# Query and key projections of an attention stage by seven half-size products, on TensorE and VectorE

## The chip, the cores and the metric

One core of one Trainium2 chip. The kernel is one launch that computes a whole inference step; its time is device microseconds. "Before" is the median of three runs, and one further execution was recorded by the hardware profiler. All arithmetic is in f32.

## The reference, cut to what matters

The step is a two-layer trunk for a prompt of 256 tokens and 8 sample tokens: a state-space mixer, experts, an attention mixer, experts, a norm. The change is in the attention mixer's projections.

```python
ATTN_PATTERNS = ((128, 1), (512, 4), (2048, 16))     # window, dilation
qkv = (h @ w_qkv).reshape(nb, L, N_ATTN_GROUPS, 3, ATTN_HEADS, ATTN_HEAD_DIM)
...
for g, (window, dil) in enumerate(ATTN_PATTERNS):
    q, k, v = qkv[:, :, g, 0], qkv[:, :, g, 1], qkv[:, :, g, 2]
    # prompt: band attention over own residue sequence; sample: over cached keys and the own one
    k_all = jnp.concatenate([buf[:, :, 0], k], axis=1)
    s = jnp.einsum('bshd,bskhd->bshk', q, k_all[:, idx]) * ATTN_SCALE
    ...
    rows.append(jnp.stack([k, v], axis=2))           # new keys and values are outputs too
y = combine_groups(outs, lams) @ w_out
```

`h` has 264 rows (256 prompt, 8 sample) of 1024, and `w_qkv` is 1024 x 9216.

## The kernel before

Activations lie channel-first: `hT` is 128 partitions x 8 channel blocks x 264 tokens. Weights stream from HBM over SyncE's queue into `ring`, six buffers of 2 MB (L669 issues those of attention); one buffer holds 512 output columns, four tiles of 128.

Attention runs in three patterns `g` of 24 tiles `i`: 8 of queries, 8 of keys, 8 of values. `qkv_tile` (line L1523) makes one tile: 8 `pe.matmul` over the channel blocks, 128 weights columns by 264 tokens, into bank `i % 2`; ScalarE's `copy_tile` (L2081, L2084; for patterns 1 and 2 with the tokens re-ordered into four lanes) copies it to `qT`, `kT` or `vT`, and counts `q_e`. The profiler records each f32 `pe.matmul` as two matmuls and two weight loads.

Behind each key tile stands `rows_job`: two transposes (L930) that turn keys back into rows, which ScalarE's `copy_rows` (L2112) copies to `KV` and GpSimd stores to the outputs (L920, L922). Job 0 of a pattern turns the sample queries (L1545); GpSimd stores them to HBM (`sample_queries`, L891), to spread them to all partitions afterwards.

In the value part, step `t` is: `scores(g, t)` (L1570) of two heads, `qkv_tile` of value tile `t` with the next row job in its middle, then `lagging(g, t)`, which does the transposes and value products of earlier heads. VectorE's part of a step is `masked` (L2732 to L2747: scale, mask, maxima), ScalarE's `exps` (L2125), VectorE's `taken_up` (L2774 to L2779). `scores(g, t)` waits until the masks of step `t - 1` are done. ScalarE's order in a step is exponents, copied rows, value tile.

The sample tokens' scores over cached keys are 20 jobs on VectorE, `cache_scores(u)`: a product of keys and queries (L2790) and a reduction (L2795), 1024 elements wide. 16 jobs are of patterns 0 and 1; the last four, of pattern 2, do two batches each. Jobs 0 to 10 run at the start of VectorE's pattern 1, jobs 11 to 19 at the start of its pattern 2, and behind them stand `own_scores(g)` (L2716) and the pattern's masks:

```python
for u in range(0, NS + EARLY_JOBS) if g == 1 else range(NS + EARLY_JOBS, len(CJOBS)) if g == 2 else ():
    cache_scores(u)
own_scores(g)
```

GpSimd issues their transfers in order: `keys(u)` (L857) when job `u - 3` is done, `query(u)` (L866) when the product of job `u - 2` is done. In pattern 1 it issues those of jobs 0 to 7, then stores the new queries and waits for that store, then issues jobs 8 to 10. In pattern 2 it issues jobs 11 to 15 and the keys of 16 to 18, stores the new queries, waits, and issues the queries of 16 to 19.

Behind attention, SyncE's queue streams the experts' weights of layer 1 (L541); its first loads wait for counts that TensorE gives at value tile 71, at the transposes of the last step and in `attention_out` (L1768).

## Time and profile before

| | |
|---|---|
| median of 3 runs | 1605.45 us (1604.89 to 1606.84) |
| profiled execution | 1606.77 us, its span 1604.7 us |
| TensorE matmuls busy | 1523.1 us, 95% of the span |
| VectorE, ScalarE, GpSimd busy | 590.1, 441.0, 132.1 us |
| attention | about 750 to 1108 us |
| granted TensorE clock, mean | 0.987 |

In a row of the timeline the first number is the start in us from the span's start and the second the time from the first start to the last end of the instructions merged in it; what stands in brackets is the idle time of the engine before it and what ended that.

### The profile page before, as it was taken

The page shows a single profiled execution, that of the slowest core. Times are in us where ns is not written, and L with a number is a line of the kernel's source. Part 1 is how long each engine was busy: PE and PEld are TensorE (multiplying, and loading weights), DVE is VectorE, ACT ScalarE, POOL GpSimd, SP SyncE. Part 2 cuts the span into 40 slices and gives each one's busy share as a digit, 9 for nine tenths or more (in the row PEclk, how much of TensorE's full clock was granted, in tenths as well). Part 3 has the DMA queues.
Part 4 walks back from the last instruction along what each step waited for, and adds up shares of the span by engine and source line. Part 5 has one row for each costly group of instructions (what it writes and reads, how often), then busy time and mean ns, then how long its engine had stood idle before and what let it go on. Part 6 is the DMA issues. An engine that isn't in the chain of part 4 may idle for free.

```text
span 1604.7 us, 23562 instructions
## 1 busy us (share of the span) xinstructions
PE 1523.1 (95%) x9111; PEld 856.0 (53%) x9111; DVE 590.1 (37%) x1380; ACT 441.0 (27%) x1232; POOL 132.1 (8%) x286
## 2 busy tenths in 40 slices
PE   9999899999998898999999999999999999898897
PEld 6877777533333333335877878766643333333232
DVE  4589983322122222214033544544421322122123
ACT  3488871211111111112143142231311111111112
POOL 1222231100000000001001202230000000000000
PEclk9999999999999999999999999999999999999999
DMA  9678776899999999999534958697899999999996
GB/s 341 219 231 270 238 240 272 294 422 414 427 424 427 428 424 429 426 423 396 191 130 143 346 170 257 170 267 300 325 424 382 426 426 424 430 425 426 428 424 258
DMA packets 112620, 542.35 MB, mean 338 GB/s; under 512 B 9452, under 2 KB 34228, under 8 KB 80242
## 3 DMA queue, kind: packets, MB, share of 16 engines
q1 hardware_dynamic: 95414, 485.20, 75.1%
q0 software_dynamic: 16800, 55.53, 11.6%
q8 instruction: 63, 1.03, 0.3%
q10 hardware_dynamic: 316, 0.37, 0.1%
q14 instruction: 27, 0.22, 0.0%
HBM read 524.81 MB, written 16.45 MB: 337 GB/s over the span
## 4 chain that ended last, share of the span: by engine, by line
PE 60%; DMA 23%; DVE 10%; ACT 3%; issue 2%; SPq 1%; POOL 0%; DVEq 0%; ACTq 0%; POOLq 0%
PE bank L1118 19%; DMA ring<-in_moe_w_gate_up 15%; PE bank L1523 10%; PE bank L1140 10%; DMA arena<-in_moe_w_gate_up 4%; PE bank L1452 4%; PE bank L1425 3%; PE bank L930 3%; DMA arena<-sample_queries 2%; PE bank L1103 2%; PE bank L1768 2%; PE bank L1129 2%; DVE arena L2636 2%; ACT arena L2125 1%; PE bank L1155 1%
## 5 line engine op out<-in xcount | busy, mean ns | idle before, releaser
L1118 PE MATMUL bank<-ring,arena 128*64 128x512 f32 x1536 | 344.3, 602 | 30.0 <-DMA ring<-in_moe_w_gate_up 30.0
L1523 PE MATMUL bank<-hT,ring 128*128 128x264 f32 x1152 | 273.5, 391 | 0.0
L1118 PEld LDWEIGHTS bank<-ring,arena 128*64 128x64 f32 x1536 | 114.2, 138 | 255.4 <-issue 251.0
L1523 PEld LDWEIGHTS bank<-hT,ring 128*128 128x128 f32 x1152 | 214.4, 191 | 38.7 <-issue 3.7
L2471 DVE TENSOR_TENSOR arena<-arena,bank 128x512 f32<-128x512 f32 x32 | 34.4, 1074 | 429.0 <-ACT arena L1896 429.0
L1140 PE MATMUL bank<-ring,arena 128*32 128x512 f32 x1536 | 169.8, 594 | 3.5 <-ACT arena L1899 1.7
L1896 ACT ACTIVATE arena<-bank 128x512 f32<-128x512 f32 x32 | 19.1, 597 | 440.5 <-PE bank L1118 440.5
L1118 PE MATMUL bank<-arena 128*64 128x512 f32 x512 | 118.4, 615 | 15.3 <-DMA arena<-in_moe_w_gate_up 15.3
L1140 PEld LDWEIGHTS bank<-ring,arena 128*32 128x32 f32 x1536 | 49.9, 110 | 106.2 <-issue 101.5
L2412 DVE SCALAR_TENSOR_TENSOR arena<-arena 128x1024 f32<-128x1024 f32 x30 | 38.5, 1284 | 179.6 <-ACT arena L1907 179.6
L2402 DVE TENSOR_TENSOR X<-X,bank 128x512 f32<-128x512 f32 x128 | 80.5, 680 | 41.9 <-PE bank L1129 41.9
L1118 PEld LDWEIGHTS bank<-arena 128*64 128x64 f32 x512 | 40.2, 141 | 91.2 <-issue 68.9
L1425 PE MATMUL bank<-hT,ring 128*128 128x264 f32 x384 | 88.6, 387 | 0.0
L930 PE MATMUL bank<-ident,arena 128*128 128x128 f32 (+7 forms) x465 | 75.4, 272 | 10.9 <-DVE arena L2607 6.5
L930 PEld LDWEIGHTS bank<-ident,arena 128*128 128x128 f32 (+7 forms) x465 | 52.6, 138 | 54.2 <-issue 19.6
L1425 PEld LDWEIGHTS bank<-hT,ring 128*128 128x128 f32 x384 | 72.3, 190 | 12.6 <-issue 0.6
L1129 PE MATMUL bank<-arena 64*128 64x512 f32 x256 | 67.9, 628 | 0.0
L1905 ACT ACTIVATE arena<-bank 128x512 f32<-128x512 f32 x32 | 19.1, 597 | 152.5 <-PE bank L1140 152.5
L1374 PE MATMUL bank<-hT,ring 128*128 128x264 f32 x256 | 60.5, 390 | 0.0
L1452 PE MATMUL bank<-arena,ring 128*128 128x264 f32 x256 | 59.4, 392 | 0.0
L1103 PEld LDWEIGHTS bank<-arena 128*128 128x128 f32 x448 | 53.0, 193 | 10.6 <-issue 10.6
L1140 PE MATMUL bank<-arena 128*32 128x512 f32 x448 | 57.7, 593 | 0.0
(368 smaller groups left out, 1609.3 us busy)
## 6 DMA issues: line engine op xcount, KB each, us to landing
ring<-in_moe_w_gate_up SPq DMA_DIRECT2D x56, 2048.0 KB, 25.8
ring<-in_moe_w_down SPq DMA_DIRECT2D x44, 2048.0 KB, 26.5
ring<-in_moe_w_gate_up SPq DMA_DIRECT2D x76, 1024.0 KB, 20.4
arena<-in_moe_w_gate_up SPq DMA_DIRECT2D x28, 2048.0 KB, 26.3
ring<-in_attn_qkv SPq DMA_DIRECT2D x18, 2048.0 KB, 11.8
arena<-in_moe_w_down SPq DMA_DIRECT2D x28, 1024.0 KB, 26.0
ring<-in_ssm_in_proj SPq DMA_DIRECT2D x10, 2048.0 KB, 15.9
arena<-in_cache_kv_w POOLq DMA_DIRECT2D x20, 512.0 KB, 8.8
```

The lines of the kernel that those rows point to most:

```text
L930: return pe.transpose(out, in_, ident[0:in_.shape[0], 0:in_.shape[0]])
L1103: mm = pe.matmul(out[:, c, :, t, :], xn_e[:, t, d * P:(d + 1) * P], Pm[:, t, :, :], start=True, stop=True)
L1118: mm = pe.matmul(bank[j][e * SLOTS:(e + 1) * SLOTS, :], Xg[:, 4 * half + k, 2 * (p % 2) + e, :], weights(2 * half + e, p)[:, k, j * DE:(j ...
L1129: pe.matmul(bank[b][:, :], CmT[r, :], ysl[r, q, :], start=True, stop=True).then_inc(s.sc, 1)
L1140: mm = pe.matmul(bank[2 + q][o:o + HALF, :], actT[:, k, i:i + HALF], down_rows(e, p, k, kept_used)[:, q * 512:(q + 1) * 512], start=(k == ...
L1374: mm = pe.matmul(bank[0][:, 0:T], wv[:, k, (t % 4) * P:(t % 4 + 1) * P], hT[:, k, :], start=(k == 0), stop=(k == DT - 1))
L1425: mm = pe.matmul(b[:, 0:T], wv[:, k, (i % 4) * P:(i % 4 + 1) * P], hT[:, k, :], start=(n == 0), stop=(n == DT - 1))
L1452: mm = pe.matmul(bank[OUT_BANK[0][d]][:, 0:T], wv[:, k, (d % 2) * P:(d % 2 + 1) * P], conv_out[:, k, :], start=(k == 0), stop=(k == XT_TIL ...
L1523: mm = pe.matmul(bank[i % 2][:, 0:T], wv[:, k, (i % 4) * P:(i % 4 + 1) * P], hT[:, k, :], start=(n == 0), stop=(n == DT - 1))
L2402: return v.tensor_tensor(xs, xs, bank[b][:, :], ALU.add)
L2412: v.scalar_tensor_tensor(out=acc_s[:, :, :], in0=ysl[:, :, :], scalar=wcol[:, bass.ds(n, 1)], in1=acc_s[:, :, :], op0=ALU.mult, op1=ALU.ad ...
L2471: v.tensor_tensor(act_r[:, :].rearrange("s (k p) -> s k p", k=4), sg[:, :].rearrange("s (p k) -> s k p", k=4), bank[1][:, :].rearrange("s ...
```

## The change

In each pattern the query and key tiles are taken in pairs `(i, i + 1)`, all but the first two of pattern 0 and the first four of patterns 1 and 2: 19 of 24 pairs. A pair is a product of 264 x 1024 tokens with 1024 x 256 weights; it is cut in halves in each of the three sizes and made of seven products of halves (Strassen's scheme in the form with 15 sums) in place of eight. A half product is 4 `pe.matmul` of 128 weight columns by 132 tokens.

- VectorE makes four sums of token halves once (`x_sums`), and four sums of weight quarters for each pair (`weight_sums`), 128 x 512 each; one is written over the quarter in `ring`.
- TensorE (`qkv_pair`) makes the seven products in two banks, some of them accumulating on others; it waits ahead of each for copies, additions and sums. Two row jobs stand inside the pairs of keys behind the first.
- ScalarE (`copy_pair`) copies three partial products to SBUF and the last result to its place; VectorE (`add_pair`) adds the other three results, 128 x 132 each.
- VectorE's order in patterns 1 and 2 is new: two cached jobs in pattern 1, one in pattern 2; the first pair's weight sums; then for each pair its additions, the next pair's sums, one cached job (in pattern 2 only up to job 15); then the jobs that are left, `own_scores`, the masks.
- Pattern 0's mask code stands behind the first sums. The sums lie in `X`, in the cached rows' buffers (`rows_in`) in pattern 0 and in `sm` and `pT` afterwards; the masks of patterns 1 and 2 are 128 columns wide in place of 384. GpSimd's order isn't changed.

```diff
+PAIRED = tuple(24 * g + i for g in range(3) for i in range(4 if g else 2, 2 * DT, 2))
+HT_ = T // 2
+PART0, ADD0, COPY0, SUM0 = CT, CT, DI // P, DI // P
...
+        masks = [m(3 * P), m(P), m(P)]
+        x_sum4 = m(DT // 2, T // 2)
+        idle_rows = X.rearrange("p t d -> p (t d)")
+        x_sums = [idle_rows[:, s * DT // 2 * HT_:(s + 1) * DT // 2 * HT_].rearrange("p (k t) -> p k t", k=DT // 2)
+                  for s in range(3)] + [x_sum4]
+        partial = idle_rows[:, 3 * DT // 2 * HT_:(3 * DT // 2 + 3) * HT_].rearrange("p (s t) -> p s t", s=3)
+        w_room = [[rows_in.rearrange("p s d -> p (s d)")[:, b * 12 * P:(b + 1) * 12 * P] for b in range(2)],
+                  [sm.rearrange("p a b c -> p (a b c)"), pT.rearrange("p a b c d -> p (a b c d)")]]
...
+        def partial_banks(i):
+            first = (i // 2 + (i < 24)) % 2
+            q, r = bank[first], bank[1 - first]
+            return q[:, 0:HT_], r[:, 0:HT_], r[:, 2 * P:2 * P + HT_]
+        def w_sum(i, s):
+            room = w_room[i >= 24][PAIRED.index(i) % 2].rearrange("p (s k n) -> p s k n", s=3, k=DT // 2)
+            return room[:, s]
...
+            def qkv_pair(i, jobs):
+                n = PAIRED.index(i)
+                q, r, p = partial_banks(i)
+                summed = SUM0 + 8 + 4 * (n - 1)
+                if i % 4 == 0:
+                    slot = (STREAM_SLOT[1] + i // 4) % RING
+                    pe.wait_ge(loads[1][slot], 16 * (i // 4 // RING + 1))
+                def product(out, ws, xs, more=False):
+                    for k in range(DT // 2):
+                        mm = pe.matmul(out, ws[:, k, :], xs[:, k, :], start=(k == 0 and not more),
+                                       stop=(k == DT // 2 - 1), skip_group_check=more)
+                    return mm
+                if n:
+                    pe.wait_ge(s_cv, ADD0 + 3 * n)
+                pe.wait_ge(q_e, i - 1 if i - 2 not in PAIRED else i - 2)
+                product(q, quarter_of(i, 0, 0), tokens_of(0, 0)).then_inc(s_prj, 1)
+                pe.wait_ge(q_e, i)
+                pe.wait_ge(s_xdt, summed + 2 if n else SUM0 + 3)
+                product(r, quarter_of(i, 0, 1), x_sums[0]).then_inc(s_prj, 1)
+                if jobs:
+                    rows_job(*jobs[0])
+                pe.wait_ge(s_zc, COPY0 + 3 * n + 1)
+                pe.wait_ge(s_xdt, summed + 3 if n else SUM0 + 5)
+                product(q, w_sum(i, 0), x_sums[1], True).then_inc(s_prj, 1)
+                pe.wait_ge(s_zc, COPY0 + 3 * n + 2)
+                pe.wait_ge(s_xdt, summed + 3 if n else SUM0 + 6)
+                product(r, quarter_of(i, 1, 1), x_sums[3], True).then_inc(s_prj, 1)
+                pe.wait_ge(s_zc, COPY0 + 3 * n + 3)
+                pe.wait_ge(s_xdt, summed + 3 if n else SUM0 + 7)
+                product(q, w_sum(i, 1), x_sums[2], True).then_inc(s_prj, 1)
+                if jobs:
+                    rows_job(*jobs[1])
+                pe.wait_ge(s_cv, ADD0 + 3 * n + 1)
+                product(p, quarter_of(i, 1, 0), tokens_of(0, 1)).then_inc(s_prj, 1)
+                pe.wait_ge(s_cv, ADD0 + 3 * n + 2)
+                pe.wait_ge(s_xdt, summed + 4 if n else SUM0 + 8)
+                product(q, w_sum(i, 2), tokens_of(1, 1), True).then_inc(q_p, 2)
...
-                for t in range(DT):
+                for t in range(4 if g else 2):
                     qkv_tile(24 * g + t, (g - 1, 2 * DT) if g == NGRP - 1 and t == 0 else None)
                     if g and t < 2:
                         lagging(g - 1, DT + t)
                     elif g == 1 and t == 2:
                         sums_to_lanes()
-                for t in range(DT):
-                    qkv_tile(24 * g + DT + t)
-                    if g == 0 and t == 0:
+                for i in range(4 if g else 2, 2 * DT, 2):
+                    j = i - DT - 1
+                    qkv_pair(24 * g + i, ((g, j), (g, j + 1)) if j > 0 else None)
+                    if i == DT:
                         pe.wait_ge(c_v, 1)
-                    rows_job(g, t)
+                        rows_job(g, 0)
                 for t in range(DT):
                     scores(g, t)
+                    if t == 0:
+                        rows_job(g, DT - 1)
                     qkv_tile(24 * g + 2 * DT + t, (g, DT + t) if g else None)
                     lagging(g, t)
...
+            def copy_pair(i, jobs):
+                n = PAIRED.index(i)
+                q, r, p = partial_banks(i)
+                parts = partial
+                if n:
+                    act.wait_ge(s_cv, ADD0 + 3 * n)
+                act.wait_ge(s_prj, PART0 + 6 * n + 1)
+                act.activation(parts[:, 0], q, ACT.Copy).then_inc(s_zc, 1)
+                act.wait_ge(s_prj, PART0 + 6 * n + 2)
+                act.activation(parts[:, 1], r, ACT.Copy).then_inc(s_zc, 1)
+                if jobs:
+                    copy_rows(*jobs[0])
+                act.wait_ge(s_prj, PART0 + 6 * n + 3)
+                act.activation(parts[:, 2], q, ACT.Copy).then_inc(s_zc, 1)
+                if jobs:
+                    copy_rows(*jobs[1])
+                act.wait_ge(q_p, i + 2)
+                act.wait_ge(s_cv, ADD0 + 3 * n + 3)
+                for out, part in projected(i, 1):
+                    ins = act.activation(out, part(q), ACT.Copy)
+                ins.then_inc(q_e, 2)
...
+            halves_summed = [SUM0]
+            def half_sum(out, x, y, op):
+                halves_summed[0] += 1
+                v.tensor_tensor(out, x, y, op).then_inc(s_xdt, 1)
+            def sums_done():
+                v.wait_ge(s_xdt, halves_summed[0])
+            def weights_landed(i):
+                slot = (STREAM_SLOT[1] + i // 4) % RING
+                v.wait_ge(loads[1][slot], 16 * (i // 4 // RING + 1))
+                n = PAIRED.index(i)
+                if n >= 2:
+                    v.wait_ge(q_p, PAIRED[n - 2] + 2)
+            def weight_sums(i, step):
+                b11, b12, b21, b22 = (quarter_of(i, r, c) for r in range(2) for c in range(2))
+                t2, t3, t4 = (w_sum(i, j) for j in range(3))
+                if step == 0:
+                    half_sum(t3, b22, b12, ALU.subtract)
+                elif step == 1:
+                    half_sum(b12, b12, b11, ALU.subtract)
+                elif step == 2:
+                    half_sum(t2, b22, b12, ALU.subtract)
+                else:
+                    half_sum(t4, b21, t2, ALU.subtract)
+            def all_weight_sums(i):
+                weights_landed(i)
+                for step in range(4):
+                    weight_sums(i, step)
+                    if 0 < step < 3:
+                        sums_done()
+            def added(i, r, x, y):
+                for out, part in projected(i, r):
+                    ins = v.tensor_tensor(out, part(x), part(y), ALU.add)
+                ins.then_inc(s_cv, 1)
+            def add_pair(i):
+                n = PAIRED.index(i)
+                q, r, p = partial_banks(i)
+                parts = partial
+                v.wait_ge(s_zc, COPY0 + 3 * n + 3)
+                v.wait_ge(s_prj, PART0 + 6 * n + 4)
+                added(i + 1, 0, r, parts[:, 2])
+                v.wait_ge(s_prj, PART0 + 6 * n + 5)
+                added(i + 1, 1, q, parts[:, 1])
+                v.wait_ge(s_prj, PART0 + 6 * n + 6)
+                added(i, 0, p, parts[:, 0])
+            v.wait_ge(n_ht, HT_BASE[2] + DT)
+            half_sum(x_sums[0], tokens_of(1, 0), tokens_of(1, 1), ALU.add)
+            weights_landed(PAIRED[0])
+            weight_sums(PAIRED[0], 0)
+            weight_sums(PAIRED[0], 1)
+            sums_done()
+            half_sum(x_sums[1], x_sums[0], tokens_of(0, 0), ALU.subtract)
+            weight_sums(PAIRED[0], 2)
+            sums_done()
+            half_sum(x_sums[3], tokens_of(0, 1), x_sums[1], ALU.subtract)
+            half_sum(x_sums[2], tokens_of(0, 0), tokens_of(1, 0), ALU.subtract)
+            weight_sums(PAIRED[0], 3)
...
-                for u in range(0, NS + EARLY_JOBS) if g == 1 else range(NS + EARLY_JOBS, len(CJOBS)) if g == 2 else ():
+                jobs = list(range(0, NS + EARLY_JOBS) if g == 1 else range(NS + EARLY_JOBS, len(CJOBS)) if g == 2 else ())
+                ahead = 2 if g == 1 else 1
+                for u in jobs[:ahead]:
+                    cache_scores(u)
+                jobs = jobs[ahead:]
+                if g:
+                    all_weight_sums(24 * g + 4)
+                for i in range(4 if g else 2, 2 * DT, 2):
+                    add_pair(24 * g + i)
+                    if i + 2 < 2 * DT:
+                        all_weight_sums(24 * g + i + 2)
+                    if jobs and (g == 1 or jobs[0] < 2 * NS):
+                        cache_scores(jobs.pop(0))
+                for u in jobs:
                     cache_scores(u)
```

## Rows read from the trace of the kernel before

**Rows 1.** Page, parts 1, 2 and 5: engine (its matmuls); GB/s of 40 slices; groups.

```profile
PE 1523.1 (95%) x9111; PEld 856.0 (53%) x9111; DVE 590.1 (37%) x1380; ACT 441.0 (27%) x1232; POOL 132.1 (8%) x286
...
GB/s 341 219 231 270 238 240 272 294 422 414 427 424 427 428 424 429 426 423 396 191 130 143 346 170 257 170 267 300 325 424 382 426 426 424 430 425 426 428 424 258
...
L1523 PEld LDWEIGHTS bank<-hT,ring 128*128 128x128 f32 x1152 | 214.4, 191 | 38.7 <-issue 3.7
...
L930 PE MATMUL bank<-ident,arena 128*128 128x128 f32 (+7 forms) x465 | 75.4, 272 | 10.9 <-DVE arena L2607 6.5
```

**Rows 2.** Timeline, SyncE's queue after attention: start us, us, what was issued.

```profile
1094.94 4.19 SPq L541 DMA_DIRECT2D ring<-in_moe_w_gate_up  x4
```

**Rows 3.** Windows: stretch, its length, each engine's busy us (instructions), clock, DMA.

```profile
880.90:925.80 44.90, 44.90 (x209) 37.72 (x207) 22.46 (x19) 7.69 (x34) 10.25 (x19) 1.00 0.95 347
987.75:1032.60 44.85, 44.85 (x209) 37.71 (x207) 19.44 (x16) 7.65 (x33) 11.58 (x22) 1.00 0.88 248
1100.79:1104.68 3.89, 3.89 (x14) 2.96 (x10) 1.29 (x3) 0.00 (x0) 0.00 (x0) 0.50 1.01 423
```

**Rows 4.** The chain that ended last, in order of time, attention's pattern 2.

```profile
1007.72 7.91 DMA sample_queries<-X
```

**Rows 5.** Timeline, TensorE: start us, us from first start to last end, count.

```profile
73.16 0.83 PE L1354 MATMUL bank<-arena 128*128 128x128 f32 x6
...
788.87 3.73 PE L1523 MATMUL bank<-hT,ring 128*128 128x264 f32 x16
```

**Rows 6.** Groups of 750 to 1110 us by form, VectorE: busy us, mean ns.

```profile
L2790 DVE TENSOR_TENSOR arena<-arena 128x1024 f32<-128x1024 f32 x20 | 24.5, 1226 | 49.5 <-DMA arena<-sample_queries 49.4
L2795 DVE TENSOR_REDUCE arena<-arena 128x16 f32<-128x1024 f32 x16 | 19.5, 1221 | 0.6
...
L2760 DVE TENSOR_TENSOR arena<-arena 128x256 f32<-128x256 f32 x8 | 3.3, 417 | 0.0
```

**Rows 7.** Waits, 750 to 1110 us: who for whom, us, times, longest.

```profile
DVE arena L2716 <- ACT arena L2084: 54.1, 1, 54.1
```

**Rows 8.** Timeline, VectorE: start us, us, operation, idle before it and releaser.

```profile
878.17 1.23 DVE L2790 TENSOR_TENSOR arena<-arena 128x1024 f32<-128x1024 f32 x1 [0.55 <-DMA arena<-sample_queries]
...
885.00 1.23 DVE L2790 TENSOR_TENSOR arena<-arena 128x1024 f32<-128x1024 f32 x1 [1.85 <-DMA arena<-sample_queries]
...
927.53 0.22 DVE L2716 TENSOR_TENSOR arena<-arena 128x64 f32<-128x64 f32 x1
...
1003.94 1.23 DVE L2790 TENSOR_TENSOR arena<-arena 128x1024 f32<-128x1024 f32 x1 [3.42 <-DMA arena<-sample_queries]
...
1020.78 1.23 DVE L2790 TENSOR_TENSOR arena<-arena 128x1024 f32<-128x1024 f32 x1 [14.37 <-DMA arena<-sample_queries]
...
1036.47 0.23 DVE L2716 TENSOR_TENSOR arena<-arena 128x64 f32<-128x64 f32 x1
```

**Rows 9.** Timeline, TensorE, at the scores L1570 and in the clock's dip.

```profile
925.84 0.46 PE L1570 MATMUL bank<-arena 64*64 64x64 f32 x16
...
930.76 0.46 PE L1570 MATMUL bank<-arena 64*64 64x64 f32 x16
...
1037.60 0.46 PE L1570 MATMUL bank<-arena 64*64 64x64 f32 x16
...
1100.79 3.89 PE L1768 MATMUL bank<-arena,ring 128*128 128x264 f32 x8
```

**Rows 10.** Timeline, GpSimd: issues of cached keys, queries and the queries' store.

```profile
879.70 0.53 POOL L866 DMA_DIRECT2D arena<-sample_queries  x1 [7.24 <-DVE arena L2790]
...
902.00 0.61 POOL L891 DMA_DIRECT2D sample_queries<-X  x1
908.95 0.54 POOL L857 DMA_DIRECT2D arena<-in_cache_kv_w  x1 [6.34 <-DMA sample_queries<-X]
```

**Rows 11.** DMA issues by line: count, KB each, median us from issue to landing.

```profile
arena<-sample_queries POOLq DMA_DIRECT2D x16, 512.0 KB, 7.9
```

**Rows 12.** Timeline, ScalarE, pattern 1, the copy that waits for the stored rows.

```profile
936.67 0.39 ACT L2112 ACTIVATE arena<-bank 128x256 f32<-128x256 f32 x1 [2.01 <-DMA out<-X]
```

More of the change, by code:

```diff
@@ L274, in bass_hybrid_step @@
         pT = m(2, 2, 3, P)
-        mask = m(NGRP, 3 * P)
         rows_in = m(CSLOTS, D)
@@ L828, in _ @@
             for g in range(NGRP):
-                link(pool.memset(mask[:, g, :], 0.0))
+                link(pool.memset(masks[g], 0.0))
                 for c0, c1, base in ((0, P, 0), (P, 3 * P, P)) if g == 0 else ((0, P, 0),):
-                    v_ = mask[:, g, c0:c1]
+                    v_ = masks[g][:, c0:c1]
                     link(pool.affine_select(out=v_, in_=v_, compare_op=ALU.is_ge, fill=NEG, base=base,
@@ L2164, in _ @@
             for g in range(NGRP):
-                for t in range(DT):
+                for t in range(4 if g else 2):
                     if g == NGRP - 1 and t == 0:
@@ L2170, in _ @@
                         lagging(g - 1, DT + t)
-                own_columns(g, 0)
-                for t in range(DT):
-                    copy_tile(g, DT + t)
-                    copy_rows(g, t)
+                for i in range(4 if g else 2, 2 * DT, 2):
+                    j = i - DT - 1
+                    if i == DT:
+                        own_columns(g, 0)
+                    copy_pair(24 * g + i, ((g, j), (g, j + 1)) if j > 0 else None)
+                    if i == DT:
+                        copy_rows(g, 0)
+                copy_rows(g, DT - 1)
                 own_columns(g, 1)
@@ L2696, in _ @@
+            weight_sums(PAIRED[0], 3)
             v.wait_ge(s_const, 9)
-            v.tensor_copy(mask[:, 0, 0:1], mask[:, 0, 0:1]).then_inc(a_mv, 1)
+            v.tensor_copy(masks[0][:, 0:1], masks[0][:, 0:1]).then_inc(a_mv, 1)
             dist, rest, apart = pT[:, 0, 0, 0, :], pT[:, 0, 1, 0, :], sm[:, 0, 0, 0:P]
@@ L2703, in _ @@
                 link(v.tensor_scalar(apart, apart, 0.0, NEG, ALU.not_equal, ALU.mult))
-                link(v.tensor_tensor(mask[:, g, 0:P], mask[:, g, 0:P], apart, ALU.min))
-                v.tensor_copy(mask[LQ:P, g, 0:LQ], mask[LQ:P, g, LQ:P]).then_inc(a_mv, 1)
+                link(v.tensor_tensor(masks[g][:, 0:P], masks[g][:, 0:P], apart, ALU.min))
+                v.tensor_copy(masks[g][LQ:P, 0:LQ], masks[g][LQ:P, LQ:P]).then_inc(a_mv, 1)
             v.wait_ge(a_mv, 3)
@@ L2736, in masked @@
                         v.scalar_tensor_tensor(out=s_[:, h, :], in0=bank[2 + h][:, 0:3 * P], scalar=SCALE,
-                                               in1=mask[:, g, :], op0=ALU.mult, op1=ALU.add).then_inc(h_m, 1)
+                                               in1=masks[g][:, :], op0=ALU.mult, op1=ALU.add).then_inc(h_m, 1)
                 v.wait_ge(h_m, 2 * n + 2)
```

25 lines of the change are left out of this document (20 added, 5 removed).

## The prediction

> **What bounds the kernel now.** I read the page first. TensorE is busy 95% of the span, and its projection line L1523 stands there with 1152 weight loads, one ahead of each matmul, two matmuls for each `pe.matmul` of the code [rows 1]. The row of GB/s shows where DMA is the limit: the slices of both expert stages stand at 380 to 430, those of attention at 130 to 350. So attention, about 750 to 1108 us, is TensorE's, and the expert stage behind it is a stream that starts when attention gives up its buffers: the queue's first expert load of layer 1 goes out at 1094.94 [rows 2]. A shift of attention's end moves everything behind it by as much, and a shift inside attention is what has to be found.
>
> Then the table of windows, for the two stretches that hold the paired tiles of patterns 1 and 2: TensorE is busy for all of both, at granted clock 1.00, and VectorE for half (22.5 of 44.9 us, 19.4 of 44.85) [rows 3]. That half is the cached key jobs. TensorE being full hides that VectorE's half is itself nearly on the path: the chain that ended last runs in pattern 2 not through TensorE but through the transfers of the cached jobs, 7.91 us for the store of the new queries among them [rows 4]. What VectorE's program does last before the value tiles decides when these can go on.
>
> **The change, term by term.**
>
> *The products.* A run of 6 matmuls with 128 columns lasts 0.83 us, one of 16 with 264 columns 3.73 [rows 5]. A single one of 128 lasts 0.27 (line L930 [rows 1]), so they start (0.83 - 0.27)/5 = 0.11 us apart and drain for 0.16 after that; for 264 it is (3.73 - 0.16)/16 = 0.223. For 132 columns I take 0.1125 (the row of 128 gives 0.11, a line between the two 0.115). One product is 4 `pe.matmul`, 8 matmuls, 0.90 us; a pair is 7 products, 6.30 us, in place of 32 x 0.223 = 7.12. If nothing waits the gain is 0.82 us a pair, 15.6 us for 19: the most the change can bring.
>
> In all the rows that these steps come from a weight load (0.19 us each [rows 1]) stands ahead of every matmul and adds nothing to the step; for 132 columns I see no reason for another case. The Trainium skill (TensorE: Matmul & The Clock Gate, Part 3, The mechanism) says that a weight load overlaps a running matmul only where it goes to another row group. By that rule the load would lie open and the change would be dear; this trace doesn't agree, since the steps of 0.11 and 0.223 hold the loads already.
>
> *Each product's wait.* Ahead of a product TensorE waits for a copy or an addition of the product before last, so each has one product, 0.90 us, of cover. A drain (0.17), a 132-column copy or addition (VectorE's 256-column form takes 0.417 and the 1024-column one 1.226 [rows 6], so about 0.29 for 132, and I take 0.39 where the columns go to lanes) and the way back (about 0.1) make 0.6 to 0.7: hidden. The closest one is the second product of the next pair, which wants two weight sums: 0.20 after the sixth product the last addition starts, 0.30 for it, then 0.60 and 0.69 (512 columns between the same two forms), together 1.84 against 1.80. I take 0.04 a pair.
>
> *Pattern 0* (7 pairs): VectorE has nothing else here (its first wait for a copied tile is 54.1 us [rows 7]). 6 x (7.12 - 6.34) + 0.82 = **-5.5 us**. The mask code, some 4 us of small steps, now stands behind eight sums of some 5 us, and is through about when the first addition is wanted.
>
> *Pattern 1, to the end of the key tiles.* VectorE does two cached jobs, then the sums of the first pair. A job is 1.226 + 1.221 and a step between, 2.49 us [rows 6]. They start at 878.17 [rows 8] (all times here as before, without pattern 0's gain), end at 883.15, two sums are there at 884.45. TensorE comes to pair 28 at 880.9, where the first stretch of [rows 3] begins, and wants the second product at 881.8: a stall of 2.7. The sixth product ends at 889.0. From then on VectorE sets the pace, for between two pairs it has addition 0.30, sums 2.64 (0.60 + 0.72 + 0.72 + 0.60), job 2.50, addition 0.39, and then TensorE's sixth product 0.90 and its drain and the ways 0.25: 6.98 us, above TensorE's own 6.30 (6.74 with two row jobs). Five such steps: 923.9, and the key tiles end at 924.8 instead of 925.84 [rows 9]. Six pairs bring 1.0 us.
>
> *The jobs left over.* Eleven jobs are due; two go ahead and six between, so three more stand behind the last pair's one, and `own_scores` and the masks behind them. Job 7 runs 924.4 to 926.9. Queue order on GpSimd sets the rest. `query(7)` waits for job 5's product, now about 914.3 (pair 34's sixth product 909.9, addition and sums 3.1, product 1.23). Behind it on GpSimd is the store of the new queries, which takes from 902.00 to 908.95 now [rows 10], so 915.0 to 922.0; behind that keys and query 8, and queries 9 and 10 wait for jobs 7 and 8. A query lands 7.9 us after its issue [rows 11]: job 8 930.4 to 932.9, job 9 933.6 to 936.1, job 10 (issued 931.7) 939.6 to 942.1. `own_scores` was at 927.53 [rows 8], so its masks are **14.6 us late**. TensorE reaches the second scores at 930.8 in either kernel (now 930.76 [rows 9]) and can go no further. Now there are 2.6 us between the masks and those scores; they don't help much, because masks, exponents, copied rows, their store and the next rows are one chain whose end holds TensorE's rows job at 937.6: ScalarE waits 2.01 us for that store and copies at 936.67 [rows 12], half a microsecond ahead of need. So 14.6 - 0.5 = **+14.1 us**, with the 1.0 swallowed. From there the value steps go on at their old 5.8 us.
>
> *Pattern 2.* The first pair has its sums in time (job 11 ends at 985.6; the pair starts at 987.75 with the second stretch of [rows 3] and wants the second product at 988.65). Four steps of 6.98, two of TensorE's: the key tiles end 3.6 us early, at 1028.8. But job 15, that started at 1003.94 and ended at 1006.4 [rows 8], now stands behind pair 58 (sixth product 993.15 + 3 x 6.98 = 1014.1, addition and sums 3.1) and ends at 1019.7. `keys(18)` waits for it, behind that on GpSimd the store of the new queries and behind that `query(16)`. Now it is 14.4 us from job 15's end to job 16's start at 1020.78, and 15.7 more for the four jobs on 128 partitions to `own_scores` at 1036.47 [rows 8]; nothing in either changes. So `own_scores` comes at 1049.8, 13.3 us late; I take **+13.1 us**, for the store's issue had waited 0.2 for the rows as well. TensorE's second scores, at 1037.60 [rows 9], are already less than 1 us behind the masks, and its next rows wait: no slack.
>
> *The clock.* TensorE will stand still some 10 and 15 us. After a gap in the small steps at 1098 the trace shows the granted clock at 0.50, which is 1.2 GHz [rows 3]: 8 matmuls of 264 columns in 3.89 us [rows 9], some 1.9 lost. This lies here under the chains of masks and stores just named; I take 0 and keep 2 x 1.9 for the range.
>
> **Sum.** -5.5 + 14.1 + 13.1 = +21.7 us. The profiled execution took 1606.77 us (span 1604.7), so 1628.5 by its own time; it lies 1.3 above the median of the runs, which gives **1627**.
>
> **Rivals.**
> (a) *The late masks are covered*, and only the products count: 15.6 less 2.7 and less 3.9 for VectorE's pace (4 steps by 0.68, 5 by 0.24), 9 us faster, 1596. For it: TensorE has other work behind the key tiles (value tile and rows job, 5 us). Against: VectorE's program is in order, and even with every transfer landed it has four jobs of 2.49 and four of 3.73, 10 and 15 us, ahead of masks that TensorE wants 5.3 us later. It decides only if a tail is under 5.3 us. 0.05.
> (b) *The transfers are quick and the tail is VectorE alone in pattern 1*: `own_scores` at 924.4 + 4 x 2.49 = 934.4, +6.4 in place of +14.1; with pattern 2 at +12 (a store like pattern 1's 6.95 us) it is +13, 1618. For it: a query that landed 5.3 us after its issue (879.70 [rows 10], 885.00 [rows 8]). Against: the median. 0.12.
> (c) *The waits between products are open*: if each of 7 x 19 ways costs 0.1 more than its cover, 13 us more, 1640. For it: margins of 0.2 to 0.3. Against: row jobs with their waits now stand between tiles and add nothing. 0.07.
> (d) *The weight load lies open* by the rule above, 0.19 a matmul: a pair 56 x 0.19 = 10.6 us dearer, 200 us in all. Only the Trainium skill's sentence speaks for it, each of the steps above against it. 0.01.
> (e) *No change*: the gains and the late masks cancel, 1605. The gain can't pass 15.6 and 10.5 of delay in pattern 2 alone are hard to avoid. 0.03.
>
> **How the numbers follow.** My own case has 0.72. Its own range takes landings from the 5.3 us of (b) to as much above the median (-4, +3), the pace at 6.7 to 7.3 us (9 steps, of which late jobs feel about 3 each, -2, +2) and the clock (0, +3.8): 1619 to 1635. With (b) and part of (c) inside, 1614 to 1637 for 8 in 10. About 0.2% (3.2 us) is what a measurement of this kernel can tell from no change. Faster by more: 0.05; within: 0.03; slower by more: 0.92.
>
> **What would show it.** L1523's pairs in steps of 0.112 to 0.114 us; the interval between like products of neighbouring pairs 6.3 to 6.4 in pattern 0 and about 7.0 where a cached job lies between; TensorE idle about 10 us ahead of the second scores of pattern 1 and about 15 ahead of those of pattern 2, put down to VectorE's masks; `own_scores` of patterns 1 and 2 behind jobs 10 and 19. I am wrong if the steps are near 0.2, if VectorE reaches the masks within 5 us of the last pair, or if a gap of 10 us is there and the expert stream starts no later.

## The result and the profile after

The changed kernel takes 1625.49 us (median of 4 runs, 1624.25 to 1631.82), the kernel before 1605.17 beside it (4 runs, 1602.56 to 1606.84): ratio 1.0128, interval [1.0102, 1.0155]. Its profiled execution took 1624.25 us, span 1622.2, against 1606.77 and 1604.7. Slower, as forecast (1627, range 1614 to 1637). One kernel of the experiments, late3, had two of its six runs far longer than the others (2203.92 and 3307.87 us) in a slow state; its figures below are of the other four.

The page of the changed kernel, busy time and the line of the whole tile (L1565), which had 1152 matmuls [rows 1].

```profile
PE 1514.9 (93%) x9567; PEld 866.5 (53%) x9567; DVE 661.8 (41%) x1529; ACT 448.3 (28%) x1258; POOL 132.2 (8%) x286
L1565 PE MATMUL bank<-hT,ring 128*128 128x264 f32 x544 | 139.1, 406 | 0.0
```

TensorE fell from 95% to 93% of a longer span: it has less to do and waits more. VectorE took on 72 us (590.1 to 661.8). The table of windows for the first stretch of [rows 3], the pairs of pattern 1, shows where it is: 36.35 us busy in 44.90, for 22.5 before (columns: stretch, its length, busy time of PE, PEld, DVE, ACT, POOL, granted clock, DMA share, GB/s).

```profile
880.90:925.80 44.90, 44.37 (x376) 42.04 (x375) 36.35 (x60) 10.01 (x39) 7.29 (x14) 1.00 0.85 296
```

Next TensorE's timeline around the first two pairs of pattern 0; L1585 is a product of halves.

```profile
761.28 1.06 PE L1585 MATMUL bank<-hT,ring 128*128 128x132 f32 x8
762.18 1.06 PE L1585 MATMUL bank<-X,ring 128*128 128x132 f32 x8
...
774.94 1.14 PE L1585 MATMUL bank<-X,ring 128*128 128x132 f32 x8
...
781.36 1.14 PE L1585 MATMUL bank<-X,ring 128*128 128x132 f32 x8
```

Products start 0.90 us apart and the second products of neighbouring pairs 6.42, in place of 7.12 for two whole tiles. Pattern 1, the same engine, answers to [rows 9]: the open start, one sixth product, and what comes behind the key tiles (L1653 is the scores).

```profile
880.35 1.14 PE L1585 MATMUL bank<-X,ring 128*128 128x132 f32 x8 [1.88 <-DVE ring L2813]
...
886.86 1.14 PE L1585 MATMUL bank<-X,ring 128*128 128x132 f32 x8
...
890.90 1.17 PE L1585 MATMUL bank<-hT,ring 128*128 128x132 f32 x8 [0.20 <-DVE arena L2846]
...
921.18 0.46 PE L1653 MATMUL bank<-arena 64*64 64x64 f32 x16
...
937.66 0.71 PE L1653 MATMUL bank<-arena 64*64 64x64 f32 x16 [11.14 <-DVE arena L2910]
938.30 3.89 PE L1565 MATMUL bank<-hT,ring 128*128 128x264 f32 x8
```

The first scores come 4.7 us earlier than in the kernel before, at 921.18 for 925.84 (3.5 of it from pattern 0); the second stand 11.14 us for the masks (L2910) and start at 937.66 for 930.76. The value tile behind them takes 3.89 us in place of 2.05, at half clock. VectorE, the same place: L2968 is a cached job's multiplication, L2894 `own_scores` [rows 8].

```profile
920.70 1.22 DVE L2968 TENSOR_TENSOR arena<-arena 128x1024 f32<-128x1024 f32 x1
...
923.93 1.23 DVE L2968 TENSOR_TENSOR arena<-arena 128x1024 f32<-128x1024 f32 x1 [0.76 <-DMA arena<-sample_queries]
...
930.48 1.23 DVE L2968 TENSOR_TENSOR arena<-arena 128x1024 f32<-128x1024 f32 x1 [4.07 <-DMA arena<-sample_queries]
...
934.51 1.23 DVE L2968 TENSOR_TENSOR arena<-arena 128x1024 f32<-128x1024 f32 x1 [1.55 <-DMA arena<-sample_queries]
...
936.90 0.22 DVE L2894 TENSOR_TENSOR arena<-arena 128x64 f32<-128x64 f32 x1
```

Of the 16.2 us from job 7 to the own scores 9.8 are work and 6.4 waits for query rows. Pattern 2: GpSimd's store and what waits for it (against [rows 4]), then VectorE's jobs 16 and 19 and the own scores, then TensorE's second scores.

```profile
1030.32 1.03 POOL L899 DMA_DIRECT2D arena<-in_cache_kv_w  x2 [6.28 <-DVE arena L2973]
1031.33 0.61 POOL L933 DMA_DIRECT2D sample_queries<-X  x1
1035.14 2.05 POOL L908 DMA_DIRECT2D arena<-sample_queries  x4 [3.19 <-DMA sample_queries<-X]
```

```profile
1040.97 1.23 DVE L2968 TENSOR_TENSOR arena<-arena 128x1024 f32<-128x1024 f32 x1 [2.04 <-DMA arena<-sample_queries]
...
1052.49 1.23 DVE L2968 TENSOR_TENSOR arena<-arena 128x1024 f32<-128x1024 f32 x1 [0.34 <-DMA arena<-sample_queries]
1056.22 0.22 DVE L2894 TENSOR_TENSOR arena<-arena 128x64 f32<-128x64 f32 x1
```

```profile
1056.99 0.71 PE L1653 MATMUL bank<-arena 64*64 64x64 f32 x16 [12.32 <-DVE arena L2910]
```

The chain that ended last says the same in one view: from the job behind pair 34 (job 5, at 909.36) it runs through VectorE, the store and two landings, and comes back to TensorE only behind the masks. (A landing is the time from a transfer's issue to its arrival.)

```profile
909.36 1.23 DVE arena L2968
...
911.39 6.17 DMA sample_queries<-X
...
918.37 5.46 DMA arena<-sample_queries
923.93 1.24 DVE arena L2968
...
925.45 8.96 DMA arena<-sample_queries
934.51 1.24 DVE arena L2968
```

The queue's first expert load [rows 2] follows:

```profile
1114.14 4.21 SPq L583 DMA_DIRECT2D ring<-in_moe_w_gate_up  x4
```

To see where the time goes I cut each kernel's timeline at four marks: TensorE's first query tile of pattern 0, its `sums_to_lanes` at the start of pattern 1 (16 small matmuls that bring pattern 0's running maxima and sums to lane order; L1615 before, L1698 after), job 11's start on VectorE (the first job of pattern 2), and the first expert load (at 1094.94 before, at 1114.14 after). In us, from the timelines of the profiled executions:

| kernel | pattern 0 | pattern 1 | pattern 2 | 1 and 2 | span |
|---|---|---|---|---|---|
| before | 126.76 | 106.22 | 111.84 | 218.06 | 1604.7 |
| after | 122.67 | 119.48 | 121.30 | 240.78 | 1622.2 |
| difference | -4.1 | +13.3 | +9.5 | +22.7 | +17.5 |

The first mark lies 0.6 later in the changed kernel and the stretch behind the last one is 1.7 shorter (508.06 for 509.76): -4.1 + 13.3 + 9.5 + 0.6 - 1.7 = 17.6, the difference of the spans within rounding.

### The profile page after: what moved, and what is told of

It reads as the page before. It is cut to its first block, busy times and chain, and to the rows that moved or that the text cites. A ratio compares the mean times of both kernels' runs of the same rounds, so it can differ in the third digit from the quotient of the medians.

```text
span 1622.2 us, 24823 instructions
## 1 busy us (share of the span) xinstructions
PE 1514.9 (93%) x9567; PEld 866.5 (53%) x9567; DVE 661.8 (41%) x1529; ACT 448.3 (28%) x1258; POOL 132.2 (8%) x286
## 4 chain that ended last, share of the span: by engine, by line
PE 59%; DMA 22%; DVE 12%; ACT 3%; issue 3%; SPq 1%; POOL 0%; DVEq 0%; ACTq 0%
PE bank L1160 19%; DMA ring<-in_moe_w_gate_up 15%; PE bank L1182 10%; PE bank L1565 5%; PE bank L1585 4%; DMA arena<-in_moe_w_gate_up 4%; PE bank L1494 4%; PE bank L1467 3%; PE bank L972 3%; PE bank L1145 2%; PE bank L1854 2%; PE bank L1171 2%; DVE arena L2749 2%; DMA arena<-sample_queries 2%; ACT arena L2234 1%
## 5 line engine op out<-in xcount | busy, mean ns | idle before, releaser
L1565 PE MATMUL bank<-hT,ring 128*128 128x264 f32 x544 | 139.1, 406 | 0.0
L1565 PEld LDWEIGHTS bank<-hT,ring 128*128 128x128 f32 x544 | 103.8, 198 | 20.7 <-issue 2.8
L1467 PE MATMUL bank<-hT,ring 128*128 128x264 f32 x384 | 88.6, 387 | 0.0
L1467 PEld LDWEIGHTS bank<-hT,ring 128*128 128x128 f32 x384 | 72.3, 190 | 12.6 <-issue 0.6
L1416 PE MATMUL bank<-hT,ring 128*128 128x264 f32 x256 | 60.0, 388 | 0.0
## 6 DMA issues: line engine op xcount, KB each, us to landing
ring<-in_moe_w_gate_up SPq DMA_DIRECT2D x76, 1024.0 KB, 20.3
```

Of the source, the lines that this page charges most:

```text
L1416: mm = pe.matmul(bank[0][:, 0:T], wv[:, k, (t % 4) * P:(t % 4 + 1) * P], hT[:, k, :], start=(k == 0), stop=(k == DT - 1))
L1467: mm = pe.matmul(b[:, 0:T], wv[:, k, (i % 4) * P:(i % 4 + 1) * P], hT[:, k, :], start=(n == 0), stop=(n == DT - 1))
L1565: mm = pe.matmul(bank[i % 2][:, 0:T], wv[:, k, (i % 4) * P:(i % 4 + 1) * P], hT[:, k, :], start=(n == 0), stop=(n == DT - 1))
```

## The experiments

**One pattern at a time.** `p0`, `p01` and `p02` keep the new code, but take whole tiles, with the cached jobs ahead of the own scores as before, in the patterns that are not named.

```diff
-PAIRED = tuple(24 * g + i for g in range(3) for i in range(4 if g else 2, 2 * DT, 2))
+WITH_PAIRS = (0,)      # (0, 1) in p01, (0, 2) in p02
+PAIRED = tuple(24 * g + i for g in WITH_PAIRS for i in range(4 if g else 2, 2 * DT, 2))
...
+                for t in () if all_paired else range(DT):
+                    qkv_tile(24 * g + DT + t)
+                    rows_job(g, t)
```

p0: 

> Pairs in pattern 0 alone (7 of 19); patterns 1 and 2 as before. If the loss comes from the cached jobs that stand between and behind the pairs, nothing of it is here: 4 to 5.5 us faster than before, 1600 us, VectorE's own_scores of patterns 1 and 2 earlier by that. If the seven products with their waits are the loss, this is not faster, some 0 to 3 us slower.

p01: 

> Pairs in patterns 0 and 1 (13 of 19). Late cached jobs: own_scores of pattern 1 about 9 us later than before, the stage behind it 13 to 14 us later than with pattern 0 alone, 1613 to 1614 us. Costly products: 6 more pairs cost what 7 cost, so a step of at most a few us.

p02: 

> Pairs in patterns 0 and 2 (13 of 19). Late cached jobs: 9 to 13 us above pattern 0 alone, 1609 to 1613 us; with the run of patterns 0 and 1 the steps add up to the whole change, 1625. Costly products: a step of a few us, as in pattern 1.

| kernel | median us (runs) | ratio to before | pattern 0 | pattern 1 | pattern 2 | span |
|---|---|---|---|---|---|---|
| p0 | 1600.13 (5) | 0.9956 [0.9940, 0.9972] | 121.41 | 106.61 | 114.70 | 1600.1 |
| p01 | 1619.36 (6) | 1.0084 [1.0062, 1.0107] | 121.32 | 122.44 | 109.81 | 1611.6 |
| p02 | 1613.55 (8) | 1.0038 [1.0019, 1.0057] | 122.73 | 106.41 | 121.49 | 1616.7 |

Pairs in pattern 0 alone are faster than both kernels. Each of the other patterns loses where it has the pairs and only there, 15.8 us in pattern 1 and 6.8 in pattern 2 against p0, each with its wait ahead of the second scores, p01 first:

```profile
938.04 0.71 PE L1654 MATMUL bank<-arena 64*64 64x64 f32 x16 [12.12 <-DVE arena L2922]
```

```profile
1048.40 0.71 PE L1654 MATMUL bank<-arena 64*64 64x64 f32 x16 [11.59 <-DVE arena L2922]
```

A caution on single executions: the stretch of pattern 2 without pairs lies at 109.8 to 114.7 us in before, p0 and p01, and p01's profiled execution is 6 us under its median. The profiled executions of p02, narrow_after and late8_store, too, lie 5 us over, 5 over and 6 under their medians. Differences under 3 us between stretches of two kernels carry nothing here.

p01 came 5 us above the 1613 to 1614 that were expected, p02 half a microsecond above its range. The two steps over p0 add up to a ratio of 1.0166 where all pairs together measured 1.0128; the intervals of the four ratios span that difference, so whether the losses overlap stays open.

**Is it VectorE's work?** The cached jobs cut to 16 columns, once in the kernel before and once in the changed one; all transfers and waits stay. (The scores of the sample against the cached keys are left out by this.)

```diff
-                v.tensor_tensor(kk, kk, rows_in[0:r, slot, :], ALU.mult).then_inc(k_m, 1)
+                v.tensor_tensor(kk[:, 0:DT * 2], kk[:, 0:DT * 2], rows_in[0:r, slot, 0:DT * 2], ALU.mult).then_inc(k_m, 1)
...
-                    ins = v.tensor_reduce(out, kk[p].rearrange("p (t h d) -> p t h d", h=2, d=HD), AX, ALU.add)
+                    ins = v.tensor_copy(out, kk[p, 0:DT * 2].rearrange("p (t h) -> p t h", h=2))
```

narrow_before: 

> Before, with each cached key job cut to 16 columns (some 0.4 us in place of 2.49, its transfers kept; the sample scores are then not computed). Late cached jobs: only the short waits of pattern 2 go, 2 to 4 us faster than before, 1602.

narrow_after: 

> The changed kernel with the same cut. Late cached jobs: pairs run in 6.4 us in every pattern; pattern 2 has no wait at its second scores; in pattern 1 one of some 7 us is left, from the transfers' order. 1598 us, 2 to 8 us faster than the cut kernel before. Costly products: still some 15 to 20 us slower than the cut kernel before.

Measured: narrow_before 1602.83 (10 runs), ratio 0.9981 [0.9965, 0.9997]; narrow_after 1613.19 (10 runs), 1.0040 [1.0022, 1.0058]. I had looked for 1598 in the second and missed it by 15. With narrow jobs the pairs cost 10.4 us (1613.19 for 1602.83) in place of 20.3; this rest stays with a VectorE that has nearly nothing to do. The narrow changed kernel's VectorE, jobs 8, 9 and 10 and the own scores, then TensorE's second scores of patterns 1 and 2:

```profile
926.68 0.18 DVE L2968 TENSOR_TENSOR arena<-arena 128x16 f32<-128x16 f32 x1 [3.64 <-DMA arena<-sample_queries]
...
932.65 0.17 DVE L2968 TENSOR_TENSOR arena<-arena 128x16 f32<-128x16 f32 x1 [5.57 <-DMA arena<-sample_queries]
...
937.01 0.17 DVE L2968 TENSOR_TENSOR arena<-arena 128x16 f32<-128x16 f32 x1 [3.98 <-DMA arena<-sample_queries]
...
937.31 0.22 DVE L2894 TENSOR_TENSOR arena<-arena 128x64 f32<-128x64 f32 x1
```

```profile
938.07 0.71 PE L1653 MATMUL bank<-arena 64*64 64x64 f32 x16 [9.57 <-DVE arena L2910]
...
1049.99 0.71 PE L1653 MATMUL bank<-arena 64*64 64x64 f32 x16 [6.46 <-DVE arena L2910]
```

13.2 us of waits for three landings, and TensorE's second scores still wait 9.57 us, and 6.46 in pattern 2 where I had expected no wait. The pairs themselves run at full speed in these two patterns (three pairs in 19.3 us), so what stays isn't theirs; the two waits together are 16.0 us. Pattern 0's gain of some 5.4 us is in both comparisons: of the 26 us that patterns 1 and 2 lose, 16 stay with narrow jobs, and by the stretches 14.4 (229.45 for 215.10) of 22.7. So the jobs' own work on VectorE is the smaller part, about two fifths, and some three fifths of the loss is order: a job tied to each pair lets GpSimd ask for the next query rows only at the pair's pace, and the store of the new queries with three more landings comes behind all of them, ahead of the masks.

**The jobs behind the masks.** If that is so, the place of the left-over jobs is what counts. A value step of pattern 1 lasts 5.8 us and VectorE idles 2.41 of it. `late3` puts jobs 8 to 10 there; `late8` puts jobs 8 to 15 there and so takes pattern 2's jobs of the second cache out of its pairs.

```diff
-EARLY_JOBS = 3
+EARLY_JOBS = 8                       # late8; 3 in late3
...
-                for u in jobs:
+                for u in jobs if g == 2 else ():
                     cache_scores(u)
                 own_scores(g)
                 for s in range(DT + 2):
...
                     if s < DT:
                         masked(g, s)
+                    if g == 1 and s and jobs:
+                        cache_scores(jobs.pop(0))
```

GpSimd's edit isn't shown. There `query(10)` and what follows stand behind the store of the key rows; in late8 pattern 2 has no job ahead of its pairs and those of its last cache begin behind the pair `i = 10`.

late3: 

> The changed kernel with pattern 1's cached key jobs 8, 9 and 10 taken from in front of its masks and put one each behind the masks of heads' steps 1, 2 and 3, where VectorE is idle for 2.41 us of a value step of 5.81 us; GpSimd stores the key rows before it issues the tenth job's query rows. All pairs of products stay. Theory (the loss of pattern 1 is the chain of query rows that stand between the last pair and the masks): VectorE comes to the own scores after job 7, at about 923.5 instead of 936.9, the second scores wait some 2 us instead of 11.1, a job of 2.45 us fits a value step's gap nearly whole, and the time falls by about 11 us, to 1614 (1611 to 1618); pattern 2 is as it was. Rival (the pairs themselves, their pace of 6.98 us and the open start, make the loss, and work moved into value steps is paid there): no more than 4 us are won, 1621 or more.

late8: 

> As late3, and pattern 1's value steps take all eight jobs of the second cache (8 to 15) instead of three, one in each of steps 1 to 8, so that pattern 2 has only jobs 16 to 19 left: none ahead of its first pair and none behind its first three, one behind each of its last three pairs, and one in front of the masks. Theory: pattern 2's first pairs run at the 6.42 us of pattern 0 instead of 6.98, its first weight sums start one job (2.5 us) earlier, and the second scores wait for one or two jobs and one landing, 3 to 6 us, instead of 12.3; with late3's gain that is some 19 to 21 us less than the changed kernel, 1605 (1601 to 1610). Rival (the pairs make the loss): 1617 or more. A third possibility: eight jobs of 2.45 us lengthen the value steps, each by up to 1 us, since a job and the rest fill a step of 5.81 us completely: then 1609 to 1613.

`p02_late8` is late8 with whole tiles in pattern 1: 

> As late8 (jobs 8 to 15 in the value steps of pattern 1, 16 to 19 in pattern 2), but pattern 1's key and query tiles whole, each by eight matmuls, as before; pairs in patterns 0 and 2 only. Theory: pattern 1 takes what it took before (106.5 us from lanes to job 11's place), pattern 0 gives its 4 us, and pattern 2's pairs, free of jobs at first, give 3 to 4 us and lose 3 to 6 us to the jobs in front of the masks: 1599 to 1602, about the kernel with pairs in pattern 0 alone (1600.1). Rival (pairs lose in themselves in lane order, whatever stands between): 1608 or more, near the 1613.6 of pairs in patterns 0 and 2 with the jobs where they were.

| kernel | median us (runs) | ratio to before | pattern 0 | 1 and 2 | span |
|---|---|---|---|---|---|
| late3 | 1619.2 (4) | 1.0086 [1.0069, 1.0104] | 121.21 | 235.51 | 1615.7 |
| late8 | 1610.02 (12) | 1.0029 [1.0013, 1.0044] | 122.69 | 226.55 | 1610.1 |
| p02_late8 | 1603.92 (12) | 0.9987 [0.9975, 1.0000] | 121.43 | 220.39 | 1601.5 |

late3 won 6.5 us by the spans, as by the ratios (1.0128 less 1.0086), where my theory had 11 and the rival no more than 4: neither was right. By stretches 7.3 of it lie in pattern 1, and pattern 2 took 2.0 more. The masks came when I had said, `own_scores` 49.7 us behind `sums_to_lanes` (50.1 expected), and no scores waited in pattern 1. But the next link of the chain took over. ScalarE and TensorE of late3 (L2234 is the copy of rows behind the stored keys, as in [rows 12]; L985 the next rows):

```profile
934.14 0.38 ACT L2234 ACTIVATE arena<-bank 128x256 f32<-128x256 f32 x1 [6.80 <-DMA out<-X]
```

```profile
935.01 0.59 PE L985 MATMUL bank<-ident,arena 128*128 128x128 f32 x2 [4.60 <-ACT arena L2180]
935.40 3.49 PE L1578 MATMUL bank<-hT,ring 128*128 128x264 f32 x8
```

The first value rows may be copied only when the stored key rows have landed, and these stores stood behind key and query loads on GpSimd. The one issued last (925.52) landed 8.6 us later, where in the kernel before it took 3.6. late8 came to 1610, at the edge of the theory's range and where its third possibility had it, but not for that reason: its value steps keep 5.8 us, and its loss is the same store (7.18 us on ScalarE, 4.98 on TensorE). In pattern 2 its second scores wait 2.41 us in place of 12.32; two products of the last pairs wait 1.11 us each behind a job of the last cache. ScalarE, then TensorE:

```profile
939.55 0.38 ACT L2234 ACTIVATE arena<-bank 128x256 f32<-128x256 f32 x1 [7.18 <-DMA out<-X]
```

```profile
940.43 0.66 PE L985 MATMUL bank<-ident,arena 128*128 128x128 f32 x2 [4.98 <-ACT arena L2180]
...
1044.38 0.46 PE L1666 MATMUL bank<-arena 64*64 64x64 f32 x16 [2.41 <-DVE arena L2923]
```

p02_late8 lies 2 us above the theory's range, as TensorE waits 2.40 us there too, and well below the rival's 1608: most of what p02 lost was the place of the jobs. That pairs in lane order cost nothing isn't shown. Against p0_late8 below, the same kernel with whole tiles in pattern 2, it is 0.0022 of the ratio slower, with intervals that just overlap, and no run here shows a gain from the pairs of pattern 1 or 2.

**The store first.** `late8_store` moves the store of the first half of the key rows directly behind the store of the queries, ahead of the wait for that.

```diff
                pool.dma_start(..., q_own).then_inc(q_st, 16)
+                if g == 1:
+                    pool.wait_ge(kv_e, JOBS * g + 5)
+                    for c in range(FOLD):
+                        pool.dma_start(folds_[c, :, :, 0, 0:512], KV[c * LQ:(c + 1) * LQ, :, 0:512]).then_inc(kvst, 16)
```

late8_store: 

> As late8, with one thing moved on GpSimd in pattern 1: the store of the first half of the key tiles (512 columns, two transfers) stands directly behind the store of the queries, ahead of the wait for the queries' landing, and no longer behind the keys and queries of jobs 8 to 10. Theory: in late8 the second scores no longer wait, but ScalarE's copy of the first value tile waits 7.18 us for the key tiles' stores, issued at 925.95 and 929.47 and landed at 939.5, TensorE waits 4.98 us behind it and then runs some 2 us at half clock. With the first half's store out of the way the last one lands some 4 us after its issue, as in the kernel before (933.04 to 936.67), TensorE waits for nothing there, and 5 to 7 us are won: 1604 (1602 to 1607). Rival (the landing takes 8 us whatever stands ahead of it): no more than 1 us, 1609 to 1611.

`p0_late8` has pairs in pattern 0 alone, with late8's jobs: 

> Pairs in pattern 0 alone, and the second cache's jobs 8 to 15 in the value steps of pattern 1 as in late8. Against the kernel with pairs in pattern 0 alone (1600.1) this moves jobs and nothing else. Theory (VectorE has the time in a value step, and where no pair needs VectorE the place of the jobs is free): 1600.1, within 2 us. Rival (jobs in the value steps cost, which would be why pairs in patterns 0 and 2 with late jobs, 1603.9, are not below pairs in pattern 0 alone): 1603 to 1606.

late8_store: 1606.96 us (12 runs), ratio 1.0007 [0.9992, 1.0021]; patterns 1 and 2 take 220.85, 5.7 less than in late8. The median fell 3.1 us, of the 5 to 7 expected; the intervals of the two ratios overlap, and the profiled execution lies 6 us under its median, so the 5.7 are partly that. ScalarE's copy waits 4.98 us instead of 7.18 and TensorE 2.82 instead of 4.98: the last store is issued at 925.19 and lands at 932.0, 6.8 us, between theory and rival. Its place in the queue need not be all of it: by the table of windows the 16 DMA engines were busy 99 to 104% of the stretch in which this store landed in late3, late8 and late8_store (8.6, 9.0 and 6.8 us), and 60 to 74% in all the others (3.6 to 4.7 us), p02_late8 and p0_late8 with late8's order on GpSimd among them (4.5 and 4.3). Earlier masks moved the store into a busier time; no run separates the two. The median is at the upper end of the theory's range. ScalarE, then TensorE:

```profile
932.02 0.38 ACT L2242 ACTIVATE arena<-bank 128x256 f32<-128x256 f32 x1 [4.98 <-DMA out<-X]
```

```profile
932.90 0.41 PE L993 MATMUL bank<-ident,arena 128*128 128x128 f32 x2 [2.82 <-ACT arena L2188]
```

p0_late8: 1599.12 us (12 runs), ratio 0.9965 [0.9948, 0.9981]: beside p0's 0.9956 the place of the jobs makes no difference where no pair needs VectorE. It is the lowest median, p0 the lowest ratio; the intervals overlap, and p0, with the fewer edits, is the version to keep. What is not explained: p0_late8 has 6 us less in patterns 1 and 2 than p0 (215.11 for 221.31) and no shorter time; its first query tile came 4.5 us later (755.39 for 750.86), before anything that was changed, and the expert stage took 2 us more.

## Why the prediction was right

The mechanism came as forecast, in both patterns: masks late behind the cached jobs, TensorE waiting for them, the expert stream later by as much. That the number is within 1.5 us is in part luck. By the profiled execution +21.7 us was forecast and +17.5 came; the terms were off by +1.4, -0.8 and -3.6 and the rest by -1.1, and the median lies 1.2 above the execution that the profile shows.

**The products: right.** 0.90 us apart, 6.42 us a pair where 6.34 was worked out; the 0.12 above seven times 0.90 is the second product's wait for the weight sums, sized at 0.04, and a sum's row reads 0.68 to 0.69 us and the next starts 0.60 to 0.73 behind it, as forecast. No weight load shows between products: eight matmuls in 0.90 us are the 0.1125 of the forecast, so rival (d) is out. The Trainium skill's rule on row groups (TensorE: Matmul & The Clock Gate, Part 3, The mechanism), that a weight load overlaps running matmuls only where the row group differs, doesn't agree with these rows: loads of 128 x 128 for the whole array, 190 ns each in the groups of L1585, stand ahead of steps of 0.1125 us.

**Pattern 0, -5.5: right in mechanism.** After gave -4.1, but the seven other kernels that share this code and whose stretch lies at 121.2 to 121.4 give -5.3 to -5.6. The other three (after, p02, late8) lie at 122.7. The table of windows gives these three a granted clock of 0.97 for 750 to 875 us and the seven 0.99 or 1.00: the 1.3 us are the clock at the stretch's start, not the change. narrow_before, which has no pairs, shows the same: 0.97, and 127.92 us for the 126.76 of before at 0.99. Like clock against like, the pairs give -5.2 to -5.6.

**Pattern 1, +14.1: +13.3.** The open start was 1.88 us of idle (2.7 forecast); like products behind it lie 6.98 us apart with a job between them (880.35 to 886.86 for the first, whose sums are early, then 886.86 to 893.85), the sum of the forecast; the step with the sample queries' transposes in it took 7.40, the next 6.88. `own_scores` came 12.9 us late against the mark (`sums_to_lanes`; 63.54 us behind it for 50.65), forecast 14.6. The store took 6.2 us and the wait for query rows 4.07 and 1.55, where 7.0 us had been put for the store and 7.9 for a landing: two landings were 5.5 and 9.0 us in the chain. The other 0.4 us of the 13.3 came behind the masks; the 0.5 us of slack that the forecast took off didn't show.

**Pattern 2, +13.1: +9.5, the term that was off.** Job 15 ended 37.2 us behind job 11's start (forecast 36.6), so the pace was right. The step that failed is "now it is 14.4 us from job 15's end to job 16's start ... nothing in either changes": it was 11.0 (1030.0 to 1040.97). In the kernel before the store of the queries was 7.91 us of the chain [rows 4], here 3.52, the landing 5.23 behind it. I had carried over this landing as a constant, and it isn't one. From this store's issue to the next issue on GpSimd the table of windows of each kernel gives, for pattern 2:

| kernels | store to next issue, us | DMA engines busy |
|---|---|---|
| before, p0, p01 (whole tiles) | 8.2, 7.7, 7.1 | 94 to 102% |
| narrow_before (whole tiles) | 6.4 | 104% |
| after, late3, p02, narrow_after (pairs) | 3.8 to 4.1 | 54 to 59% |
| p0_late8 (whole tiles) | 3.7 | 74% |
| late8, late8_store, p02_late8 (pairs) | 2.1 to 2.2 | 6 to 9% |

With pairs the store fell into a quieter time. That this made it quick is likely but not shown: no run changed the share alone, and in pattern 1 the same store took 6.5 to 7.9 us at 71 to 72% (after, late3, late8, narrow_after). Quick transfers are rival (b)'s thought; they came in the other pattern. From job 16 to the own scores it was 15.25 us for 15.7.

**What the experiments add.** The forecast gave the late masks two causes, VectorE's work and the landings, without weights. The narrow jobs show some two fifths for the work and three for the order and landings; in their profiled execution a landing took 9.8 us and the store 7.6, longer than with full jobs, so the shares are rough. Late jobs show what the argument "half a microsecond ahead of need" about the stored rows [rows 12] was worth: with the masks in time, that store is the next to hold TensorE, for 4.6 us. And patterns 1 and 2 had little to win: with a job in each pair the 6.98 us leave 0.14 of the 0.82.

**The clock.** The table of windows of the changed kernel around the first wait:

```profile
930.40:937.66 7.26, 0.00 (x0) 0.03 (x1) 5.53 (x8) 0.00 (x0) 0.00 (x0) 0.50 0.71 282
...
937.66:944.10 6.44, 6.44 (x30) 5.05 (x31) 2.47 (x12) 3.93 (x22) 1.72 (x3) 0.51 0.23 51
...
944.10:950.00 5.90, 5.90 (x45) 4.69 (x45) 1.58 (x7) 3.01 (x16) 0.00 (x0) 1.00 0.16 39
```

For the first 6.44 us of work it still stands at 0.51: two value tiles take 3.89 and 2.75 us in place of 2.05, 2.5 us in all (in pattern 2 one takes 3.25). It lies under the chain of stored rows, as forecast: ScalarE's copy behind them starts at 946.06, 9.16 us after `own_scores`, and in the kernel before 9.14 after it [rows 8, 12].

Left open: pairs in pattern 1 or 2 with no loss. late8_store comes to "no change" with pairs in all patterns; whether its last 2.8 us of wait and the 1.9 us start can be removed I didn't try, nor a store of key rows moved into a quiet time by itself.

## What to carry to other kernels

Before an idle engine is given work, ask what its program does next and who waits for that: VectorE was idle half of the time, and still the work ahead of its masks set the end of the stage. Jobs tied one to one to a slower loop pull their transfers' issue along with them, and the landings that can no longer be prefetched come one by one behind the loop. Take a trick where the helping engine has nothing else in its order (pattern 0: 7 of 19 pairs brought all of the gain), and price a landing as a range, not by its median, with an eye on how busy the DMA engines are where it will fall.

## What the runs showed of the hardware

- A 132-column f32 product with a full 128 x 128 weight load ahead of each matmul keeps 0.1125 us a step; the loads (190 ns each in the groups of L1585) add nothing to it.
- The same store of 32 KB of queries took from 2.1 us (late8, DMA engines 6% busy in its stretch) to 8.2 (before, 94%) until the next issue behind it, with 6.5 to 7.9 at 71 to 72% in between; the landings of query rows in the chains of before, after and narrow_after took 4.3 to 12.1 us. The last store of the key rows took 3.6 us in the kernel before (66% busy), 8.6 in late3 (99%), 9.0 in late8 and 6.8 in late8_store (104%).
- In a wait of 11.1 us TensorE's granted clock fell to 0.5 (1.2 GHz) and stayed there for the first 6.4 us of work behind it; eight matmuls of 264 columns took 3.89 us.
